# The decay loop of a bidirectional SSD layer: one product for a step's exponents, and dt applied in VectorE's passes

## What is computed

```python
A_cum = jnp.cumsum(A, axis=-1)                      # A = dt * a, per head and chunk of 128 tokens
scores = einsum("bclhn,bcshn->bhcls", Cc, Bc) * exp(segsum(A))
y_diag = einsum("bhcls,bcshp->bclhp", scores, xd)   # xd = x * dt
...                                                 # y_off from the chunk states, both directions
y = rmsnorm((y_f + y_b + skip) * silu(z), ssd_norm_w)
```

## Time and profile before

| what | value |
|---|---|
| median of 3 runs | 953.76 us (953.66 to 956.06) |
| the profiled execution | 954.61 us, span 952.8 us |
| TensorE busy | 855.1 us of the span (90%) |
| VectorE, ScalarE, GpSimd busy | 401.3, 162.7, 210.1 us |
| mean granted TensorE clock | 0.960 |

### The profile page before, as it was taken

One profiled execution on the slowest core, in us unless ns is written; L12 is line 12 of the kernel. 1 busy time (PEld: TensorE's weight loads), 2 busy tenths in 40 slices (PEclk: granted clock), 3 DMA queues, 4 the chain that ended last, 5 costly groups with the idle time before them and its releaser, 6 DMA issues.

```text
span 952.8 us, 18676 instructions
## 1 busy us (share of the span) xinstructions
PE 855.1 (90%) x8036; PEld 483.1 (51%) x8036; DVE 401.3 (42%) x773; ACT 162.7 (17%) x369; POOL 210.1 (22%) x255
## 2 busy tenths in 40 slices
PE   1899999999899999999999994699998999999940
PEld 1656655555554555564444442455554555555520
DVE  1430012644664589985323265632222322222227
ACT  4121001212222222221010012011111111111113
POOL 0169999600141333330000000100000000000022
PEclk9999999999899999999999997699999999999985
DMA  9942755880310000069200004399999999998427
GB/s 349 419 171 90 274 223 212 290 312 1 133 44 1 1 1 1 0 239 337 115 22 23 9 14 147 142 381 419 390 415 397 352 401 379 406 404 334 152 75 279
DMA packets 41809, 198.91 MB, mean 209 GB/s; under 512 B 6848, under 2 KB 16256, under 8 KB 24704
## 3 DMA queue, kind: packets, MB, share of 16 engines
q1 hardware_dynamic: 22032, 162.82, 43.2%
q0 software_dynamic: 6224, 22.55, 6.8%
q10 hardware_dynamic: 13472, 12.37, 4.1%
HBM read 175.66 MB, written 22.05 MB: 208 GB/s over the span
## 4 chain that ended last, share of the span: by engine, by line
PE 57%; DVE 9%; DMA 3%; issue 2%; POOL 1%; ACT 1%; ACTq 0%; DVEq 0%; POOLq 0%
PE bank L928 19%; PE bank L796 14%; PE bank L941 9%; PE bank L660 6%; DMA slot_out<-yT 2%; PE bank L918 2%; PE bank L933 1%; PE bank L698 1%; DVE ex L1629 1%; DVE xs L1682 1%; DVE xs L2009 1%; POOL ex L1436 1%; DVE ex L1645 1%; PE bank L762 1%; DMA ex<-slot_out,ri 1%
## 5 line engine op out<-in xcount | busy, mean ns | idle before, releaser
L588 PE MATMUL bank<-hT,ring 128*128 128x512 f32 (+1 forms) x640 | 178.4, 438 | 1.5 <-DMA ring<-w_ring 1.5
L588 PEld LDWEIGHTS bank<-hT,ring 128*128 128x128 f32 x640 | 95.8, 192 | 72.0 <-issue 69.8
L1930 DVE TENSOR_TENSOR bcT<-bcT,bank 128x128 f32<-128x128 f32 x51 | 14.6, 287 | 166.4 <-ACT bcT L1255 166.4
L660 PE MATMUL bank<-ring,hT 128*128 128x512 f32 x160 | 76.9, 617 | 4.5 <-DVE ex L1653 2.2
L928 PE MATMUL bank<-ex,yT 128*32 128x256 f32 x1216 | 75.8, 392 | 1.2 <-ACT yT L1265 1.2
L928 PE MATMUL bank<-ring,yT 128*32 128x256 f32 x1248 | 76.5, 387 | 0.0
L796 PE MATMUL bank<-ring,yT 128*128 128x512 f32 x160 | 70.9, 593 | 0.8 <-DVE yT L1691 0.8
L1444 POOL DMA_INDIRECT yT<-h_dram,token_of x16 | 15.5, 969 | 237.2 <-PE bank L918 220.2
L1436 POOL TENSOR_TENSOR ex<-ex,dts 128x512 f32<-128x512 f32 x40 | 44.3, 1106 | 101.6 <-ACT ex L1167 101.5
L928 PEld LDWEIGHTS bank<-ex,yT 128*32 128x32 f32 x1216 | 37.6, 113 | 28.1 <-issue 3.4
L928 PEld LDWEIGHTS bank<-ring,yT 128*32 128x32 f32 x1248 | 38.4, 111 | 26.3 <-issue 2.2
(11 more groups left out here) (311 smaller groups left out, 1228.0 us busy)
## 6 DMA issues: line engine op xcount, KB each, us to landing
ex<-w_exp SPq DMA_DIRECT2D x36, 1024.0 KB, 18.0
ring<-w_exp SPq DMA_DIRECT2D x36, 1024.0 KB, 15.7
ring<-w_ring SPq DMA_DIRECT2D x13, 2048.0 KB, 11.6
yT<-w_late SPq DMA_DIRECT2D x16, 1024.0 KB, 6.6
hT<-w_exp SPq DMA_DIRECT2D x12, 1024.0 KB, 15.8
uT<-w_exp SPq DMA_DIRECT2D x12, 1024.0 KB, 18.2
slot_out<-ex POOLq DMA_DIRECT2D x13, 512.0 KB, 16.7
ex<-x SPq DMA_DIRECT2D x5, 512.0 KB, 8.3
```

Source lines behind the costliest of these rows:

```text
L588: mm = pe.matmul(o, w[:, k, (f % 4) * P:(f % 4 + 1) * P], hT[:, k, lo:hi], start=(k == 0), stop=(k == KT - 1))
L660: mm = pe.matmul(psb[6][:, :], hT[:, k, j * P:(j + 1) * P], w[:, k, :], start=(k == 0), stop=(k == KT - 1), skip_group_check=True)
L1930: tt(ab[v % 2], sg[v % 2], psb[v % 2][:, P:2 * P], ALU.mult).then_inc(s_ac, 1)
```

## The change

1. The exponents of a step come from the mask matmul and one more matmul. The tables are written to HBM by six DMAs on ScalarE's queue, and read back by one as `pair_rows`: 120 partitions (3 parts x 40 steps) of 512 bf16 columns (two heads, two directions, 128 tokens). A matrix `pairb` with a one where a row belongs to step i picks a step's three rows. The source tokens' term leaves TensorE: it is the bias of ScalarE's Exp, one column of `ncum` for each head and direction, so `exps` becomes four instructions of 128 columns.
2. `ncum`, which was overwritten, is made anew ahead of the loop: ten small matmuls from the tables into bank 7 ahead of `project_z(0)`, copied by ScalarE.
3. GpSimd's multiplication by dt is gone. VectorE multiplies the forward half by dt (two passes of 128 columns), adds dt times the backward half (two of 128), and multiplies the sum by the C.B product (one of 256).
4. z alternates between banks 6 and 7 and so waits for the group before the last; y's transposes take the bank that is free, `turn_y` two steps later in TensorE's order, `copy_y` one step earlier in VectorE's.
5. Three semaphores become one; nothing else changes.

```diff
+        pair_rows = dts[0:3 * NJ * HG, 6:8, :].rearrange("p a b -> p (a b)")[:, 0:256].bitcast(BF16)
+        def z_bank(jg):
+            return psb[6 + jg % 2]
+        def turn_bank(jg):
+            return psb[7] if jg >= 2 * NJ - 3 else psb[6 + jg % 2]
...
@@ TensorE @@
-                if ks[0] == 0 and jg >= 1:
-                    pe.wait_ge(s_zs, jg)
+                if ks[0] == 0 and jg == 1:
+                    pe.wait_ge(s_nc, 1)
+                if ks[0] == 0 and 2 <= jg < 4:
+                    pe.wait_ge(s_zs, jg - 1)
+                if ks[0] == 0 and jg >= 4:
+                    pe.wait_ge(s_yT, jg - 3)
...
+            for d in range(2):
+                for j in range(NJ):
+                    c = j * 32 + d * H
+                    pe.matmul(psb[7][:, c:c + H], tabT[d][:, j * P:(j + 1) * P], nstackb[:, d * H:(d + 1) * H],
+                              start=True, stop=True)
             project_z(0, range(KT))
...
                 pe.matmul(o[:, :], idb[:, :], MASK4, start=True, stop=False, skip_group_check=True)
-                o4 = o[:, :].rearrange("p (h d t) -> p h d t", h=2, d=2)
-                for d in range(2):
-                    c = d * H + hh
-                    pe.matmul(o4[:, :, d, :], tabT[d][:, j * P:(j + 1) * P],
-                              nstackb[:, c:c + 2].unsqueeze(2).to_broadcast([96, 2, P]), start=False, stop=False,
-                              skip_group_check=True)
-                for q in range(4):
-                    h, d = hh + q // 2, q % 2
-                    c = d * H + h
-                    mm = pe.matmul(o[:, q * P:(q + 1) * P], stackb[:, c:c + 1].to_broadcast([96, P]),
-                                   tabT[d][:, j * P:(j + 1) * P], start=False, stop=True,
-                                   skip_group_check=True)
-                mm.then_inc(s_e, 1)
+                if i == 0:
+                    pe.wait_ge(s_tdr, 16)
+                pe.matmul(o[:, :], pairb[:, i:i + 1].to_broadcast([3 * NJ * HG, P]), pair_rows, start=False, stop=True,
+                          skip_group_check=True).then_inc(s_e, 1)
...
             def turn_y(jg):
                 pe.wait_ge(s_yc, jg + 1)
-                if jg >= 1:
+                pe.wait_ge(s_zs, min(jg + 3, 2 * NJ))
+                if jg >= 2 * NJ - 2:
                     pe.wait_ge(s_yT, jg)
...
                     if i == NS - 3:
-                        pe.wait_ge(s_zs, 2 * NJ)
+                        pe.wait_ge(s_zs, 2 * NJ - 1)
+                        pe.wait_ge(s_yT, 2 * NJ - 3)
...
-                    if k % 4 == 1 and k // 4 >= 1:
+                    if k % 4 == 3 and k // 4 >= 1:
                         turn_y(k // 4 - 1)
@@ ScalarE @@
+            def store_tables():
+                act.wait_ge(s_tabs, 2)
+                for c in range(3):
+                    for d in range(2):
+                        r = c * 32 + d * H
+                        act.dma_start(decay_rows[c].rearrange("j h d t -> h j d t")[:, :, d, :],
+                                      tabT[d][r:r + H, :].rearrange("p (j t) -> p j t", j=NJ)).then_inc(s_tdw, 16)
+            store_tables()
             for i in range(4, 8):
+                if i == 6:
+                    act.wait_ge(s_tdw, 96)
+                    act.dma_start(pair_rows, decay_rows.rearrange("c j (q h) d t -> (c j q) (h d t)", h=2)).then_inc(
+                        s_tdr, 16)
                 scale_pooled(i)
...
-                act.activation(wbuf(i)[:, :, :, :], psb[4 + i % 2][:, :].rearrange("p (h d t) -> p h d t", h=2, d=2),
-                               ACT.Exp).then_inc(s_ex, 1)
+                for q in range(4):
+                    c = j * 32 + (q % 2) * H + hh + q // 2
+                    ins = act.activation(wbuf(i)[:, q // 2, q % 2, :], psb[4 + i % 2][:, q * P:(q + 1) * P], ACT.Exp,
+                                         bias=ncum[:, c:c + 1])
+                ins.then_inc(s_ex, 1)
...
+            act.wait_ge(s_z, 1)
+            act.activation(ncum, psb[7][:, 0:160], ACT.Copy).then_inc(s_nc, 1)
+            act.wait_ge(s_nc, 1)
             tanh_z(0)
@@ GpSimd @@
-            for i in range(NJ * HG):
-                j, hh = i // HG, 2 * (i % HG)
-                pool.wait_ge(s_ex, i + 1)
-                dt_h = dt_[:, j * 32:(j + 1) * 32].rearrange("p (d h) -> p h d", d=2)[:, hh:hh + 2, :]
-                pool.tensor_tensor(wbuf(i)[:, :, :, :], wbuf(i)[:, :, :, :],
-                                   dt_h.unsqueeze(3).to_broadcast([P, 2, 2, P]), ALU.mult).then_inc(s_wd, 1)
@@ VectorE @@
-                dve.wait_ge(s_wd, i + 1)
+                dve.wait_ge(s_ex, i + 1)
...
-                step(tt(w.rearrange("p h d t -> p (h d) t"), w.rearrange("p h d t -> p (h d) t"),
-                        gT[:, j, hh // HG, :].unsqueeze(1).to_broadcast([P, 4, P]), ALU.mult))
-
-                tt(w[:, :, 0, :], w[:, :, 0, :], w[:, :, 1, :], ALU.add).then_inc(s_w, 1)
+                for q in range(2):
+                    c = j * 32 + hh + q
+                    ins = ts(w[:, q, 0, :], w[:, q, 0, :], dt_[:, c:c + 1], None, ALU.mult)
+                step(ins)
+                for q in range(2):
+                    c = j * 32 + H + hh + q
+                    ins = stt(w[:, q, 0, :], w[:, q, 1, :], dt_[:, c:c + 1], w[:, q, 0, :], ALU.mult, ALU.add)
+                step(ins)
+                tt(w[:, :, 0, :], w[:, :, 0, :], gT[:, j, hh // HG, :].unsqueeze(1).to_broadcast([P, 2, P]),
+                   ALU.mult).then_inc(s_w, 1)
...
-                if i % 4 == 1 and i >= 8:
+                if i % 4 == 0 and i >= 8:
                     copy_y(i // 4 - 2)
```

More of the change, by code:

```diff
@@ L103 @@
 C_ALL = 818
-B_STRICT, B_MASK, B_STACK, B_ALL = 0, 128, 384, 416
+B_STRICT, B_MASK, B_STACK, B_PAIR, B_ALL = 0, 128, 384, 416, 456
 XDD_ORDER = ((0, 0), (1, 0), (0, 1), (1, 4), (0, 2), (1, 3), (0, 3), (1, 2))
@@ L140, in trunk_kernel @@
         h2_dram = nc.dram_tensor("h2_dram", [TOK, D], F32).ap()
+        decay_rows = nc.dram_tensor("decay_rows", [3, NJ, H, 2, P], BF16).ap()
         slot_out = nc.dram_tensor("slot_out", [SLOTS, D], F32).ap()
@@ L164, in trunk_kernel @@
         onesb = sb("onesb", [P, P], BF16)
-        stackb = sb("stackb", [96, 32], BF16)
         nstackb = sb("nstackb", [96, 32], BF16)
@@ L272, in trunk_kernel @@
         s_hs = sem("h_ready")
-        s_dtr = sem("dt_rows_product")
-        s_dtc = sem("dt_rows_on_chip")
-        s_dtp = sem("dt_token_major")
+        s_dtr = sem("dt_handover")
         s_soft = sem("softplus_handover")
@@ L303, in trunk_kernel @@
         s_sout = sem("context_states_stored")
-        s_wd = sem("decays_times_dt")
         s_e = sem("exponents_built")
+        s_nc = sem("negated_sums_copied")
+        s_tdw = sem("decay_tables_stored")
+        s_tdr = sem("decay_rows_loaded")
         s_ex = sem("decays_exponentiated")
@@ L409, in trunk_kernel @@
         token_of = sb("token_of", [P, MAX_TILES + 1], I32)
+        pairb = token_of[0:3 * NJ * HG, 0:NJ * HG // 2].bitcast(BF16)
         gate = sb("gate", [P, 2 * NJ])
@@ L629, in _ @@
                 if f == 1:
-                    pe.wait_ge(s_dtc, 1)
+                    pe.wait_ge(s_dtr, 2)
                     for j in range(NJ):
@@ L634, in _ @@
                                        cst[:, C_STACK:C_STACK + 32], start=True, stop=True)
-                    mm.then_inc(s_dtp, 1)
+                    mm.then_inc(s_dtr, 1)
                 if f == 2:
@@ L656, in project_z @@
                     pe.wait_ge(s_ring[m % RING], 16 * (m // RING + 1))
-                if ks[0] == 0 and jg >= 1:
-                    pe.wait_ge(s_zs, jg)
+                if ks[0] == 0 and jg == 1:
[4 more added lines that the diff above has]
+                    pe.wait_ge(s_yT, jg - 3)
                 for k in ks:
-                    mm = pe.matmul(psb[6][:, :], hT[:, k, j * P:(j + 1) * P], w[:, k, :],
+                    mm = pe.matmul(z_bank(jg)[:, :], hT[:, k, j * P:(j + 1) * P], w[:, k, :],
                                    start=(k == 0), stop=(k == KT - 1), skip_group_check=True)
@@ L781, in turn_y @@
                     k = 4 * (jg % 2) + q
-                    mm = pe.transpose(psb[7][:, q * P:(q + 1) * P], xs[:, jg // 2, k * P:(k + 1) * P], ident)
+                    mm = pe.transpose(turn_bank(jg)[:, q * P:(q + 1) * P], xs[:, jg // 2, k * P:(k + 1) * P], ident)
                 mm.then_inc(s_ytr, 1)
@@ L1106, in _ @@
                     act.activation(dtrow[:, 0:CTX], psb[1][:, 0:CTX], ACT.Copy)
-                    act.activation(dtrow[:, CTX:TOK], psb[0][:, :], ACT.Copy).then_inc(s_dtc, 1)
+                    act.activation(dtrow[:, CTX:TOK], psb[0][:, :], ACT.Copy).then_inc(s_dtr, 1)
                 if f == 1:
@@ L1159, in tanh_z @@
                     act.wait_ge(s_yc, jg - 2)
-                act.activation(zbuf[jg % 3], psb[6][:, :], ACT.Tanh, scale=0.5).then_inc(s_zt, 1)
```

(15 more changed lines are left out.)

## The result

| | before | after |
|---|---|---|
| median of 4 runs | 954.72 us | 943.47 us (939.47 to 944.24) |
| ratio, 95% interval | | 0.9873 (0.984 to 0.9905) |
| the profiled execution | 954.61 us, span 952.8 | 939.47 us, span 937.6 |
| VectorE, ScalarE, GpSimd busy | 401.3, 162.7, 210.1 us | 400.7, 185.0, 164.4 us |
| group of the loop | 13.93 us | 12.39 us |

The kernel is 1.3% faster; 944.3 was predicted. The profiled execution after is the quickest of its four. The other 3.9 lie behind its start, where nothing was changed and where the profiles of this study differ by as much: 506.1 us before, 502.2 to 507.0 in the other kernels.

What follows compares the result with a forecast made beforehand. TensorE was to set the group at 12.6 us, VectorE just under at 12.5. The output projection would start at 437.2 instead of 446.67, gaining 9.5: execution 954.61 to 945.1, median 944.3, range 940.4 to 951.5.

Steps and rivals of the forecast that it cites:

- z(0) to z(4): First groups of the loop: 32.2 us of TensorE work from z(1) at 299.15, so z(4) at 331.3 instead of 339.33.
- five groups: Loop from z(4) to z(9): five groups of 12.6 us, z(9) at 394.3 in place of 409.12.
- the lag: Tail: VectorE's lag from z(9) to the start of project_part(0, 1, 1) grows from 29.2 to 32.6 us.
- the clock's fall: Tail: TensorE's clock falls once to its lower level after idling, adding 1.9 us.
- the rest 8.35: Behind the loop: the 8.35 us from project_part(0, 1, 1) to the next projection stay as before.
- Exponents of 0.44: TensorE in the loop: a step's exponents take two pieces of 0.22 us in place of 0.66, saving 0.88 a group.
- The missing 0.43: Group before the change: TensorE's work sums to 13.5 of 13.93 us; the other 0.43 is a stall at z's single bank.
- Step of 1.54: VectorE in the loop: five passes of a decay step sum to 1.52 us, taken as 1.54; a group is 12.5.
- The price of a longer step: VectorE in the loop: above a step of 1.57 us, each 0.01 us counts 31 times, from copy_y(0) to the last step.
- the first rival: VectorE's neighbouring passes don't overlap: step 1.77, group 13.4 set by VectorE, 6.2 us given back, 950.8 us; chance 0.12.
- cover: Tables' HBM round trip: the load lands by 290, first exponents come near 298.5, leaving about 8 us to spare.
- The two waits: Tail: TensorE waits some 2.0 us for the last decay step and 2.7 us for the last begin_outputs.

Runs made afterwards that it cites:

- e3: The changed kernel with z back in one bank and turn_y in the other, at the old places: 945.3 us, ratio 0.991.
- e12: The kernel before with the short exponents alone (z in one bank, GpSimd multiplies by dt): 958.1 us, ratio 1.005.
- e2: The changed kernel with GpSimd multiplying by dt again and VectorE's old two passes: 941.9 us, ratio 0.9894.
- e1: The changed kernel with the old exponents (seven matmuls, one Exp of 512 columns): 951.8 us, ratio 0.9988.
- e5: The changed kernel with a wait behind each of VectorE's four narrow passes, so no pairs overlap: 948.4 us, ratio 0.9948.
- e7: The changed kernel with ScalarE making copy_y of groups 0 to 7 in place of VectorE: 938.1 us, ratio 0.9836.
- e10: The changed kernel with ScalarE's copy_y, project_part(0,1,1) filling the tail, and GpSimd multiplying by dt again: 933.5 us, ratio 0.9812.
- e6: The changed kernel with project_part(0,1,1) in its own bank, its matmuls between the last diagonals: 938.0 us, ratio 0.9856.
- e8: The changed kernel with ScalarE's copy_y of groups 0 to 7 and project_part(0,1,1)'s matmuls around the last turn_y: 932.9 us, ratio 0.9806.

## Why the prediction was right, and where it wasn't

**The time.** 944.3 was predicted, 943.5 and 943.4 are the medians. Between z(0) and project(0,0,0) a gain of 9.8 was forecast (155.5 to 145.7); it was 11.0. Term by term: z(0) to z(4) 39.3 (39.8 predicted), five groups 62.3 (63.0), the lag 32.1 (32.6), the clock's fall 2.4 (1.9), the rest 8.35 as predicted. No term is off by more than 0.7, so the time doesn't rest on errors that cancel.

**TensorE.** Exponents of 0.44 and groups of pure TensorE work: right, 12.39 against 12.6. The sum was 0.2 too large by its two commonest terms: a z pass takes 0.43 us (0.438 predicted), a diagonal 0.39 (0.41).

**The cause of the stall: the step that failed.** "The missing 0.43 is the stall at the z bank" was read from the chain's last link, `silu_z` before z. The stall is the end of a ring that passes GpSimd and VectorE, and the bank is only one of its links. By e3 it stays away with one bank if GpSimd is out: e12's 13.68 less GpSimd's 1.08 (351.91 to 352.99) and the 0.58 by which it lengthens L1711, plus the 0.43 that VectorE's step is longer (1.50 for 1.07), works out at 12.45, level with TensorE's 12.39; the measured group is 12.41. By e2 it stays away with GpSimd in if there are two banks (VectorE then sets the group). With neither it stays (e12). The forecast stood all the same, in this by luck: the change cuts the ring at both places, which the prediction didn't know. By its own reasoning the prediction would have put the short exponents alone at a gain, where e12 is slower.

So the gain of 11 isn't a sum of parts. Between the marks the short exponents alone lose 1.5 us (e12), the rest alone wins 1.4 (e1), and both together win 11.0. All three profiles have a fall of the clock in the tail that the one before lacks; the groups, which it doesn't touch, show the same: 0.24 less (e12), 0.41 less (e1), 1.53 less with both. One engine's work (13.51) and the ring (13.92) lay 0.4 apart, and whoever shortens one meets the other.

**VectorE.** Step of 1.54 predicted, 1.50 measured; the two narrow kinds were 280 and 348 ns on average, 280 and 355 predicted from wider rows. Its group is 12.16 against 12.5: `begin_outputs` takes 3.51 with what follows (359.07 to 362.58), not the 3.67 of the earlier trace rows and a wait. The price of a longer step, 31 times what exceeds 1.57, is confirmed by e5: (1.75 - 1.57) x 31 = 5.6, measured 150.5 - 144.5 = 6.0. So the first rival's sum was right and only its condition wrong: the passes do overlap. The Trainium skill says, in "VectorE: DVE Perf Modes", section "The DRAIN you can't avoid", that in a row of eight copies a semaphore after each costs nothing extra; the rows here differ, since the pair of L1672 takes 0.60 with a wait behind each pass (e5) and 0.47 or 0.48 without.

**ScalarE and the round trip.** Four passes take 1.14 us (1.15 predicted). The tables' six DMAs were issued within 3.72 us from 271.16, the load at 278.06, and it landed 2.1 us later, far ahead of the first exponents at 297.9: hidden, as predicted, with 17 us of cover left where 8 had been counted. The `ncum` matmuls cost 0.41 (0.35 predicted).

**The tail.** Lag of 32.6 predicted, 32.1 measured; one fall of the clock at 1.9, measured 2.4 (9.55 - 7.13). Its reason, that `copy_y` ties VectorE to `turn_y`, is confirmed by e7: the lag falls to 28.1. The two waits were put at 2.0 and 2.7 us, and are 1.56 and 2.40; the clock falls within the second (1.00 from 421.2 to 422.2, 0.50 from 422.7 on). In the kernel before, the one wait listed between z(9) and the projection's part is 0.78 us, and its part went at the full clock. What the prediction didn't see is that this tail was the next 6 to 9 us to be had.

**GpSimd.** Its 44.3 us in the loop went. Where z has two banks that is worth 1.0 us up to z(9) (e2), and nothing where ScalarE makes `copy_y` (e10). The Trainium skill's "SBUF — State Buffer", section "SBUF: two separate sides", has VectorE's passes with two SBUF inputs and GpSimd exclude each other for a whole instruction. The rows of e2 agree (1.57 us, ending 0.55 behind GpSimd's). By that rule alone one would have put a gain on this part; it is small because VectorE's group lies near TensorE's 12.39 either way (12.16 in the change, 12.63 on average in e2).

## What to carry to other kernels

A wait that ends a group tells the last link of a ring, not its cause: follow the chain once round, add its pieces, and compare the sum with the busiest engine's own work. Where the two are close, edits don't add up: an edit that only shortens the engine's work, or only opens the ring, shows almost nothing, and undoing one of two parts that open the same ring makes either look spare. Ask of every gain in a loop what the engine that lags gives back behind it; work that depends on nothing late belongs there, and it keeps TensorE's clock up besides.

## What the runs showed of the hardware

- TensorE's clock fell to 0.50 in the tail of the change within the last of three waits of 1.23, 1.56 and 2.40 us, with work of 5.0 and 1.1 us between them. In e2 it fell behind one of 2.04 and was back for the part. In e6 and e8, where the stretch is filled, it stayed at 1.00, and in e7, with one wait of 1.63, too.
- A wait behind each of two like VectorE passes of 128 columns costs 0.13 us a pair (0.60 for 0.47, 0.74 for 0.61).
- A VectorE pass that starts just behind one of GpSimd's ends 0.55 us after that one's end, at 1.57 us in place of 0.68 (e2).
- Small DMAs that had taken 4.7 to 7.1 us to land were a poor guide for the tables' load: 2.1 us.
